# Dense products of a hybrid decoder step: chunk of tokens outside, input slice inside, in place of slice outside, chunk inside

## What is computed

```
def _layer(x, pe, attend, ...):
    h = _rms_norm(x, g_mix)
    q, k, v, xb, yb, ga, gb = jnp.split(h @ w_in, SPLITS, axis=-1)
    ...
    a_out = att.reshape(bsz, t, MERGE_WIDTH).astype(x.dtype) @ w_oa
    hr, conv_new, h_last = _conv_rglru(xb, conv_prev, h0, w_conv, b_conv, ...)
    b_out = (hr.astype(x.dtype) * jax.nn.gelu(yb)) @ w_ob
    x = x + (jax.nn.sigmoid(ga) * a_out + jax.nn.sigmoid(gb) * b_out) @ w_o
    x = x + jnp.square(jax.nn.relu(_rms_norm(x, g_mlp) @ w_up)) @ w_down
    x = x + jax.nn.sigmoid(_rms_norm(x, g_ple) @ w_ple_gate) * (pe @ w_ple_in)
```

## Time and profile before

| | before |
|---|---|
| median of 3 runs | 2617.09 us (2616.27 to 2618.4) |
| span of the profiled execution | 2609.2 us |
| PE busy, weight loads busy | 2348.6 us, 2313.3 us (90%, 89%) |
| DVE, ACT, POOL busy | 901.2, 694.0, 670.5 us |
| `dense` on PE | from 1017.2 us to the end |

### The profile page before, as it was taken

The page is one execution under the profiler, slowest core; times in us unless marked ns, Lnnn a source line. Parts: engine busy times, 40 slices in busy tenths (PEclk is TensorE's granted clock), DMA queues, the critical chain, the costliest instruction groups (busy, mean ns, idle before and its releaser), DMA issues.

```text
span 2609.2 us, 35502 instructions
## 1 busy us (share of the span) xinstructions
PE 2348.6 (90%) x13651; PEld 2313.3 (89%) x13651; DVE 901.2 (35%) x1601; ACT 694.0 (27%) x1423; POOL 670.5 (26%) x478
## 2 busy tenths in 40 slices
PE   2789998998998954998897999999999999999988
PEld 0789998998998954998887999989999999999988
DVE  6355346346336424006555112322111021121154
ACT  3231232232233212325555223211011011011141
POOL 1131122113013102224432222434233133233241
PEclk7899999899898956999998999999999999999999
DMA  3212222222221222111111112211111111111112
GB/s 109 71 59 100 77 72 92 76 80 68 89 76 43 85 64 78 44 53 46 37 37 32 40 49 66 82 41 49 41 41 49 49 41 49 49 41 49 58 33 83
DMA packets 60500, 156.64 MB, mean 60 GB/s; under 512 B 8596, under 2 KB 29595, under 8 KB 57255
## 3 DMA queue, kind: packets, MB, share of 16 engines
q1 hardware_dynamic: 60360, 154.71, 18.5%
HBM read 140.19 MB, written 16.86 MB: 60 GB/s over the span
## 4 chain that ended last, share of the span: by engine, by line
PE 52%; issue 6%; POOL 2%; ACT 1%; DVE 0%; DMA 0%; POOLq 0%; ACTq 0%; DVEq 0%
PE d_ps L1156 51%; POOL w_lo L1358 1%; POOL xc_lo L1369 1%; PE d_ps L1179 0%; ACT w_hi L1255 0%; POOL g_lo L1366 0%; POOL tmp L1381 0%; PE d_tot L1165 0%; DMA p_raw<-p_t 0%; ACT xcat L1287 0%; ACT L1336 0%; DVE act_lo L1395 0%; DVE x_res L1467 0%; DVE tmp L1505 0%; DVE p_lo L1395 0%
## 5 line engine op out<-in xcount | busy, mean ns | idle before, releaser
L1358 POOL TENSOR_TENSOR w_lo<-w_raw,w_hi 128x1024 fp32r<-128x1024 f32 (+1 forms) x130 | 321.4, 2472 | 715.6 <-ACT w_hi L1255 715.6
L1156 PE MATMUL d_ps<-act_lo,w_hi 128*128 128x352 f32 x1728 | 374.5, 324 | 70.3 <-POOL w_lo L1358 65.1
L880 PE MATMUL at_proj<-qkv_hi,act_lo 128*128 128x384 f32 x864 | 344.7, 399 | 96.5 <-DVE qkv_lo L702 96.5
L1156 PE MATMUL d_ps<-act_hi,w_hi 128*128 128x352 f32 x1728 | 374.4, 325 | 0.0
L1156 PE MATMUL d_ps<-act_hi,w_lo 128*128 128x352 f32 x1728 | 372.8, 324 | 0.0
L1156 PEld LDWEIGHTS d_ps<-act_lo,w_hi 128*128 128x128 f32 x1728 | 297.2, 189 | 72.1 <-issue 64.7
L880 PE MATMUL at_proj<-qkv_hi,act_hi 128*128 128x384 f32 x864 | 331.2, 383 | 0.0
L880 PE MATMUL at_proj<-qkv_lo,act_hi 128*128 128x384 f32 x864 | 330.5, 383 | 0.0
L880 PEld LDWEIGHTS at_proj<-qkv_hi,act_lo 128*128 128x128 f32 x864 | 238.5, 276 | 98.7 <-issue 56.2
L1156 PEld LDWEIGHTS d_ps<-act_hi,w_hi 128*128 128x128 f32 x1728 | 295.4, 189 | 0.0
L1156 PE MATMUL d_ps<-b_lo,w_hi 128*128 128x352 f32 x1248 | 273.0, 327 | 24.2 <-POOL w_lo L1358 18.1
(11 more groups left out here) (213 smaller groups left out, 2609.4 us busy)
## 6 DMA issues: line engine op xcount, KB each, us to landing
w_raw<-w_stream SPq DMA_DIRECT2D x122, 512.0 KB, 3.5
qkv_raw<-w_qkv SPq DMA_DIRECT2D x12, 1536.0 KB, 6.6
vcache<-vc SPq DMA_DIRECT2D x12, 1024.0 KB, 5.0
kcache<-kc SPq DMA_DIRECT2D x16, 512.0 KB, 4.4
e_bc<-lse_dram SPq DMA_DIRECT2D x15, 528.0 KB, 5.3
x_in<-x_t SPq DMA_DIRECT2D x8, 528.0 KB, 7.7
tmp<-x_t SPq DMA_DIRECT2D x8, 528.0 KB, 3.6
y_t<-x_res SPq DMA_DIRECT2D x8, 528.0 KB, 3.9
```

What stands on the lines that cost most here:

```text
L880: ins = pe.matmul(pj[i % 3][:, 0:3 * HD], tile_cols(x, k, g, i), w[:, k], start=first, stop=last)
L1156: ins = pe.matmul(ps[s][:, c, 0:CH], w[:, slot, k0 + k], x[:, k, c * CH:(c + 1) * CH], start=k == 0 and x is lo, stop=k == nk - 1 and w is ...
L1358: pool.tensor_tensor(w_lo[:, s, 0:nk], w_raw[:, s, 0:nk], w_hi[:, s, 0:nk].bitcast(F32), ALU.subtract).then_inc(S["wlo"], 1)
```

## The change

In `product` the loop over chunks moves from the inside to the outside. Each chunk now takes all its input slices and all three pairs before the next chunk begins. The waits on `ready` stay before the first use of a slice, which is now in chunk 0 alone.

```
             pe.wait_ge(S["wlo"], BUMP + n + 1)
             pe.wait_ge(S[f"ev{s}"], BUMP + free)
-            for k in range(nk):
-                if ready is not None:
-                    pe.wait_ge(S[ready[0]], BUMP + ready[1] + k + 1)
-                for w, x in ((w_hi, lo), (w_hi, hi), (w_lo, hi)):
-                    for c in range(NCH):
+            for c in range(NCH):
+                for k in range(nk):
+                    if ready is not None and c == 0:
+                        pe.wait_ge(S[ready[0]], BUMP + ready[1] + k + 1)
+                    for w, x in ((w_hi, lo), (w_hi, hi), (w_lo, hi)):
                         ins = pe.matmul(ps[s][:, c, 0:CH], w[:, slot, k0 + k], x[:, k, c * CH:(c + 1) * CH],
                                         start=k == 0 and x is lo, stop=k == nk - 1 and w is w_lo)
             ins.then_inc(S["mm"], 1)
```

## The result

| | before | after |
|---|---|---|
| median of the runs | 2616.68 us (6 runs, 2609.0 to 2622.11) | 2625.56 us (6 runs, 2620.79 to 2632.62) |
| span of the profiled execution | 2609.2 us | 2622.3 us |

The ratio is 1.004, with a 95% interval of 1.0021 to 1.0059: the change makes the kernel slower by 5.5 to 15.4 us of 2,616.7. The forecast was 26 us slower, 2643, with a range of 2629 to 2655. The sign and the place of the waits were right, the size was not. The span grew by 13.1 us. In the runs after, a time lies 1.8 us above its own span (2624.07 and 2622.3 for the profiled one). So the 7.9 us between median and span before were not a fixed part of a run: the profiled execution of before was one of the shorter ones, and the 13.1 us contain that.

What follows compares the result with a forecast made beforehand. PE, busy 90% of the span, was taken to bound the kernel. New waits of 21.5 us, 4.5 us for the clock and 0 for the pace gave 26 us on 2617.1: 2643.1 us, range 2629 to 2655.

Steps and rivals of the forecast that it cites:

- The sign: Whole kernel: the change makes it slower, chance 0.92; faster 0.04, within 0.2% 0.04.
- Where the waits come: First products of the MLP's down part, `w_o`, `w_ple_in` and last gate: new PE waits for late slices, 21.5 us.
- the clock in the MLP: Behind the MLP's four waits: clock falling to 1.2 GHz costs 0.7 us each, 2.8 us in all.
- I take 0 for the pace: Matmuls in `dense`: the new order leaves 161.8 ns each unchanged, judged from the projection in `attention`; 0 us.
- the bound of 1.0 ns: Pace in `dense`: at most 1.0 ns gained per matmul, 9 us over 9,072; 4.5 us lost the other way.
- Rival A: Matmuls in `dense`: pace falls enough to pay for the waits, from 2.9 ns per matmul; chance 0.07.
- Rival B: Matmuls in `dense`: changing the stationary operand costs more than repeating it, 109 us, 2752; chance 0.07 for above 2656.

Runs made afterwards that it cites:

- e4: The changed kernel with the three PSUM banks taken in turn at every matmul; granted clock 0.69 in its first 500 us; span 3199.1 us.
- e9: The kernel of e7 with `b_lo` and every tile behind it laid 128 bytes further; span 2635.4 us.
- e3: The kernel before, operand order kept, with all chunks adding into PSUM bank 0 from input slice 1 on; span 2613.0 us.
- e6: Stationary operands in the order of the changed kernel, moving operands and banks in the order of the kernel before; span 2613.5 us.
- e8: The kernel of e4 run once more, three banks in turn on the changed kernel; span 2628.0 us.
- e5: Moving operands and banks in the order of the changed kernel, stationary operands in the order of the kernel before; span 2629.2 us.
- e7: The changed kernel with its pairs ordered (w_hi, hi), (w_hi, lo), (w_lo, hi), so no chunk is read twice in succession; span 2630.2 us.
- e2: The kernel before with slice still outermost, but inside it chunk by chunk with the three pairs; 2597.39 us, ratio 0.9942.

## Why the prediction was right or wrong

*Where the waits come: right.* Four for POOL `act_lo` of up to 2.9 us (forecast 3.05 each, 12.2; measured 11.6), one more for DVE `p_lo`, two for DVE `b_lo` (forecast 2.3 and 3.2, 5.5 together; measured 5.0), none in the branch gates or the up part. The argument behind it, slice 7 wanted after 21 matmuls in place of 63, is what the rows show.

*What they cost: right in kind, a little low.* The MLP's four products 19.3 us (forecast 12.2 + 2.8 = 15.0), `w_o` 16.96 - 13.28 = 3.7 (3.0), last gate 18.25 - 11.55 = 6.7 (5.4 + 1.7 = 7.1), `w_ple_in` stage 1.0 (0.9). Together 30.7 where 26 were forecast. The term that was too small is the clock in the MLP: 0.7 us per wait, by the average of the recurrent branch. All four waits came with a stretch at the low level, one of them longer, and cost about 2 each in clock.

*The pace: wrong, and this made the forecast miss.* The step that failed is "I take 0 for the pace", with the bound of 1.0 ns. It read the time above streaming (15.1 ns in `dense`, 14.1 in the projection) as a constant per matmul and compared the constants. Measured are 159.0 and 159.7 in place of 161.8: the term was 0 in the sum and 2.1 to 2.8 ns per matmul in the trace, more than twice its own bound. The same row read per column would have said what came: 174.1 ns / 384 columns x 352 = 159.6 ns for the new order. Two numbers speak for reading it so, this match and e4, where at the clock of 0.75 nothing lies above streaming. Neither proves it: no run changed the number of columns, and e9 shows that addresses alone move the pace by as much.

With the estimate of 20 us off, 30.7 - 20 = 11 us is left, against 13.1 in the span and 8.9 in the medians. The starts of the stages show how much of the 20 was there. Outside the products with losses and outside the recurrent stage, PE gained 16.7 us: 1.9 in the gate and output of attention, 2.4 in those of the recurrent branch, 1.1 in the rest of `w_o`, 9.9 in the rest of the MLP, 1.4 in the rest of the last gate. The recurrent stage took 242.6 us in place of 240.7, so 1.8 more. `dense` began 2.8 us sooner. 30.7 - 16.7 + 1.8 - 2.8 = 13.0 us, the span's difference. The recurrent stage of before was a short one: its granted clock was 0.98, after it was 0.97, and in e3 and e6, with the old pace and no new wait, it was 0.95, at 244.2 and 244.4 us.

*Why the pace fell: not by the causes weighed.* Rival A saw that a lower pace pays for the waits, and put the point for "within 0.2%" at 2.3 ns, which is what came; it was held at 0.07 and tied to the bank. The kernel ended outside 0.2% even so, because the losses were 30.7 us and not 26. e3 and e8 show that the bank has no part. Rival B, the changed stationary operand, has none either (e6): its 109 us nowhere appear. The Trainium skill (TensorE: Matmul & The Clock Gate, Part 2, step 1) describes PE's read port for the stationary operand as separate from that for the moving one, so that loads do not take from a running matmul; e6, with the stationary sequence changed and 161.9 ns, agrees as far as it goes: another sequence of loads cost nothing. The cause is the sequence of moving chunks (e5 against e6), and addresses enter (e7, e9). By what mechanism the read is slowed, and why one order can run at 158.9 or 161.1 ns behind different stalls, stays open.

*The sign* was right because the losses, 31 us, outweighed the gain; but over half of them was paid back by a gain that the sum had at nothing. That the forecast of 0.92 for slower came true owes something to luck.

## What to carry to other kernels

When a loop over slices moves inside one over chunks, each input slice is wanted sooner, by a factor equal to the number of chunks, here 3. So keep the old order in the products that follow their inputs closely, and only there: here 7 of 136 products turned a loss of 0.4% into a gain of 0.5%. Or reorder only inside a slice (e2), which needs no exception and gave the same (0.9942 against 0.9947).

Before carrying a pace over from matmuls of another width, work it out per column as well as by what lies above the streaming time, and let the bounds cover both readings; here they gave 159.6 and 160.8 ns. And price a wait of PE with the slow stretch behind it: here 11.6 us of waits cost 19.3.

## What was not expected of the hardware

- The order in which moving chunks are read changed the steady pace of 352-column fp32r matmuls between 158.9 and 161.8 ns, with the stationary sequence and the PSUM bank without effect (e3, e5, e6, e8).
- Laying `b_lo` and the tiles behind it 128 bytes further changed it from 159.0 to 161.7 ns in three of four blocks and to 160.6 in the first (e9 against e7).
- The same code settled at 158.9 ns in one block and at 161.1 in another and kept that through 16 products (e2).
- At a granted clock of 0.75 the new order of operands ran at 195.0 ns, with nothing above 352 columns at that clock, in up and down products alike (e4); at the full clock 12 to 13 ns lie on top (e8).
- PE's four waits of 2.9 us in the changed kernel each came with a stretch at 1.2 GHz. That is frequent but not certain: of the same four waits in e9 the last, 2.85 us until 2392.23, had none (granted 1.00 from 2389 to 2400 us), and its product took 14.7 us in place of 16.3. Nor had the wait of 3.39 us before.
